# Down projection in seven block products instead of eight, for three of four output pairs of its two groups of eight tiles

## The reference

```python
def swiglu(h, w_gate, w_up, w_down):
    return (jax.nn.silu(h @ w_gate) * (h @ w_up)) @ w_down
...
        x = x + swiglu(rmsnorm(x, norm3_g[l]), w_gate[l], w_up[l], w_down[l])
    return rmsnorm(x, norm_f_g)
```

## Time and profile before

| | us |
|---|---|
| median of 3 runs | 3106.22 |
| lowest, highest | 3101.51, 3106.39 |
| the profiled execution | 3112.17 |
| its span, first to last instruction | 3110.4 |
| PE busy | 2979.9 (96%) |
| DVE, ACT, POOL busy | 1486.7, 945.2, 1407.7 |
| mean granted TensorE clock | 0.977 of 2.4 GHz |
| down projection, first half | 1878.80 to 2124 |
| down projection, second half | 2844.85 to 3084.24 |

### The profile page before, as it was taken

The page is one execution under the profiler, slowest core; times in us unless marked ns, Lnnn a source line. Parts: engine busy times, 40 slices in busy tenths (PEclk is TensorE's granted clock), DMA queues, the critical chain, the costliest instruction groups (busy, mean ns, idle before and its releaser), DMA issues.

```text
span 3110.4 us, 62240 instructions
## 1 busy us (share of the span) xinstructions
PE 2979.9 (96%) x26914; PEld 2543.5 (82%) x26914; DVE 1486.7 (48%) x1859; ACT 945.2 (30%) x1615; POOL 1407.7 (45%) x979
## 2 busy tenths in 40 slices
PE   8999999899888899999999999999999899999997
PEld 7888888788778788987788888887898788888885
DVE  6332633366666642235766661125232866664113
ACT  4123212244444342334333331121232433332111
POOL 4555443335344326236545542246526554543225
PEclk9999999999999979999999999999999999999998
DMA  4433454311212212110322227324111122225512
GB/s 164 163 115 102 161 161 156 114 51 46 59 49 61 63 47 98 35 48 34 120 111 109 108 109 291 129 108 162 41 41 49 73 109 109 114 117 215 222 55 77
DMA packets 168066, 326.14 MB, mean 105 GB/s; under 512 B 46464, under 2 KB 103808, under 8 KB 162176
## 3 DMA queue, kind: packets, MB, share of 16 engines
q1 hardware_dynamic: 167808, 322.38, 29.7%
HBM read 232.15 MB, written 90.18 MB: 104 GB/s over the span
## 4 chain that ended last, share of the span: by engine, by line
PE 72%; DVE 6%; issue 2%; POOL 2%; ACT 1%; SPq 0%; DVEq 0%; DMA 0%; ACTq 0%; POOLq 0%
PE ps L1428 26%; PE ps L1979 25%; PE ps L1931 6%; PE ps L1534 2%; PE ps L1698 2%; PE ps L1700 2%; PE ps L1682 2%; PE ps L1652 1%; DVE tu L2182 1%; PE ps L1779 1%; DVE normed L2699 1%; PE ps L1583 1%; PE ps L1606 1%; PE ps L1638 1%; PE ps L1616 1%
## 5 line engine op out<-in xcount | busy, mean ns | idle before, releaser
L690 POOL TENSOR_TENSOR w_lo<-w_raw,w_hi 128x512 fp32r<-128x512 f32 x296 | 427.9, 1469 | 681.0 <-ACT w_hi L962 679.5
L1428 PE MATMUL ps<-a_hi,w_hi 128*128 128x512 f32 x1152 | 451.3, 392 | 16.3 <-DVE a_lo L2082 9.5
L962 ACT ACTIVATE w_hi<-w_raw 128x512 fp32r<-128x512 f32 x296 | 170.3, 623 | 966.7 <-PE ps L1428 864.4
L1428 PE MATMUL ps<-a_lo,w_hi 128*128 128x512 f32 x1152 | 449.2, 390 | 0.0
L2437 DVE TENSOR_TENSOR x<-ps,x 128x1024 f32<-128x1024 f32 (+1 forms) x80 | 97.9, 1224 | 563.5 <-PE ps L1428 554.0
L1428 PE MATMUL ps<-a_hi,w_lo 128*128 128x512 f32 x1152 | 355.2, 390 | 0.0
L1428 PE MATMUL ps<-b_hi,w_hi 128*128 128x512 f32 x768 | 301.0, 392 | 1.9 <-DVE x L2437 1.9
L1428 PE MATMUL ps<-b_lo,w_hi 128*128 128x512 f32 x768 | 299.8, 390 | 0.0
L1979 PE MATMUL ps<-a_hi,w_hi 128*128 128x512 f32 x672 | 266.6, 397 | 16.3 <-DVE a_lo L2509 8.6
L1428 PEld LDWEIGHTS ps<-a_hi,w_hi 128*128 128x128 f32 x1152 | 216.9, 188 | 63.4 <-DVE a_lo L2082 9.5
L1979 PE MATMUL ps<-a_lo,w_hi 128*128 128x512 f32 x672 | 265.6, 395 | 0.0
(11 more groups left out here) (328 smaller groups left out, 6424.7 us busy)
## 6 DMA issues: line engine op xcount, KB each, us to landing
w_raw<-in_weights SPq DMA_DIRECT2D x228, 512.0 KB, 3.9
hidden<-hid SPq DMA_DIRECT2D x44, 1024.0 KB, 3.9
zT<-z_out SPq DMA_DIRECT2D x44, 512.0 KB, 4.1
w_raw<-kvw SPq DMA_DIRECT2D x32, 512.0 KB, 3.3
a_hi<-hidden SPq DMA_DIRECT2D x28, 512.0 KB, 10.2
a_lo<-hidden SPq DMA_DIRECT2D x28, 512.0 KB, 11.3
suv<-zT SPq DMA_DIRECT2D x16, 512.0 KB, 4.8
x<-in_xT SPq DMA_DIRECT2D x16, 512.0 KB, 5.7
```

Source lines behind the costliest of these rows:

```text
L690: pool.tensor_tensor(low_t[:, u, part, :], w_raw[:, u, part, :], high[:, u, part, :].bitcast(F32), ALU.subtract).then_inc(S["w_lo_done"], 1)
L962: act.activation(split_into(pair)[0][:, u, part, :], w_raw[:, u, part, :], ACT.Copy).then_inc(S["w_hi_done"], 1)
L1428: mm = pe.matmul(to[:, nb, 0:w], wt[:, u, k, :], r[:, k, nb * w:(nb + 1) * w], start=(k == 0 and r is hi_in and wt is w_hi), stop=(k == kn ...
```

## The change

The three seven-product pairs per group come into the down projection, in groups 1 and 2 (g = 0, 1, DOWN = 2). Of the four pairs of a group the first is made as before, plainly, with both tiles side by side (`eights`); the other three by seven products (`sevens`), with bank and operand rules shared with the feed-forward stage (p runs on from 22 to 27). All three groups' tiles are now loaded into `a_hi`/`a_lo`, since the b buffers hold t2, t3, t4; the loads of the next group wait for the second and fourth product of the last pair of the group before.

The blocks are made of raw hidden tiles. For this the first 16 raw tiles are stored from `gate_t` to a new tensor `hidden_raw`, and a pair of raw tiles (j and j + 4 of the group) is loaded into one of two scratch buffers `scr`; `scr0` lies over `hid` and `up_t`, `scr1` over `gate_t`, `u_t` and `p5_t`. `blocks_of(j)` makes four blocks of it on DVE, and the load of j = 2 and 3 waits until the blocks of j - 2 are made. `into_x` adds the seven products up, right into x: nine DVE operations of 512 columns for a pair, in place of two of 1024. The text calls `blocks_of(j)` a unit.

```diff
+        scr = [place(f"scr{i}", [P, 2, TB], F32, OS + (4 + 8 * i) * KB) for i in range(2)]
...
+                if p < sum(FF_GROUPS[:DOWN]):
+                    sp.wait_ge(S["prod"], hf * FF_TILES + p + 1)
+                    sp.dma_start(hidden_raw[p], gate_t[:]).then_inc(S["raw_st"], 16)
...
+                    if j >= 2:
+                        sp.wait_ge(S["t_raw"], since("t_raw", T_RAW * hf + 12 + 16 * g + 4 * (j - 1)))
+                    elif j:
+                        sp.wait_ge(S["st_ev"], ev_all(hf, down_first(g) - 1))
+                    else:
+                        sp.wait_ge(S["hid_st"], since("hid_st", 16 * FF_TILES * (hf + 1)))
+                        if g:
+                            sp.wait_ge(S["t_raw"], since("t_raw", T_RAW * hf + 12 + 16 * g))
+                    f = sum(FF_GROUPS[:g]) + j
+                    for e in range(2):
+                        sp.dma_start(scr[j % 2][:, e, :], hidden_raw[f + e * KT // 2]).then_inc(S[f"scr_in{j % 2}"], 16)
...
+                for g in range(DOWN):
+                    p, d = down_first(g), PAIRS_OUT * g
+                    for j in range(0 if g == 0 else 1, KT // 2):
+                        load_scratch(g, j)
+                    for i in range(2, PAIRS_OUT + 1):
+                        used_up(p + i - 2)
+                        load_down(d + i)
+                    if g + 1 < DOWN:
+                        load_scratch(g + 1, 0)
+                    for k in range(FF_GROUPS[g + 1]):
+                        if k in (0, KT // 2):
+                            sp.wait_ge(S["st_done"], since("st_done", 7 * st(hf, p + DS - 1) + (4 if k else 2)))
+                        load_hidden(hf, g + 1, k)
+                    if g + 1 < DOWN:
+                        load_down(d + PAIRS_OUT + 1)
...
+                    dif_hi(0)
+                    dif_hi(1)
+                    high(p, 1, 5)
+                    dif_hi(2)
+                    dif_hi(3)
+                    act.activation(t2_hi[:], t2_raw[:], ACT.Copy).then_inc(S["t_hi"], 1)
+                    high(p, 2)
+                    copy_1(p)
+                    high(p, 3)
+                    copy_5(p)
+                    high(p, 4)
...
+                    for i in range(DS):
+                        if i:
+                            copy_1(p + i)
+                        if i + 1 < DS:
+                            high(p + i + 1, 0, 6)
+                        if i:
+                            copy_5(p + i)
...
                     product(p, 0, 0)
+                    if first_t is not None:
+                        pe.wait_ge(S["t_lo"], since("t_lo", T_LO * hf + first_t[0]))
                     product(p, 1, 1)
...
+                for g in range(DOWN):
+                    d, p = q_d + PAIRS_OUT * g, down_first(g)
+                    eights(d, g, range(KT), p - 2)
+                    t0 = 7 + 7 * g
+                    sevens(p, (S["st_ev"], ev_all(hf, p - 1)), (t0 + 4, t0 + 5, t0 + 6, t0 + 7))
+                    sevens(p + 1, (S["job_out"], 2 * (d + 1)), None)
+                    sevens(p + 2, (S["st_ev"], ev_all(hf, p)), None)
...
+                            dve.wait_ge(S["raw_st"], since("raw_st", 16 * (hf * 16 + min(p, 16))))
                             op = dve.tensor_tensor(gate_t[:, N1], bank(0), rstd[:, N1], ALU.mult)
...
+                        dve.tensor_tensor(t3_raw[:, j, :], b2[:, N2], b1[:, N2], ALU.subtract).then_inc(S["t_raw"], 1)
+                        if j == 0:
+                            dve.wait_ge(S["values_half"], half_open(hf, p))
+                        dve.tensor_tensor(x_dif[:, j, N2], b1[:, N2], b1[:, N1], ALU.subtract).then_inc(S["t_raw"], 1)
+                        dve.wait_ge(S["t_raw"], since("t_raw", raw0 + 4 * j + 1))
+                        dve.tensor_tensor(t2_raw[:, j, :], t3_raw[:, j, :], b1[:, N1], ALU.add).then_inc(S["t_raw"], 1)
+                        dve.wait_ge(S["t_raw"], since("t_raw", raw0 + 4 * j + 3))
+                        dve.tensor_tensor(t4_raw[:, j, :], b2[:, N1], t2_raw[:, j, :], ALU.subtract).then_inc(S["t_raw"], 1)
...
+                    dve.wait_ge(S["st_done"], since("st_done", 7 * st(hf, p - 1) + 7))
+                    blocks_of(0)
+                    blocks_of(1)
+                    weight_sum_3(p)
+                    weight_sum_1(p)
+                    blocks_of(2)
+                    dif_low(0)
+                    dif_low(1)
+                    blocks_of(3)
+                    dif_low(2)
+                    dif_low(3)
+                    dve.wait_ge(S["t_raw"], since("t_raw", raw0 + 16))
+                    low_block(t2_hi, t2_lo, t2_raw, 11 + 7 * g + 5)
+                    for u in range(2):
+                        add_x(d, u, u, False)
+                    weight_sum_4(p)
+                    weight_sum_2(p)
...
+                    low_block(t3_hi, t3_lo, t3_raw, 11 + 7 * g + 6)
+                    low_block(t4_hi, t4_lo, t4_raw, 11 + 7 * g + 7)
```

More of the change, by code:

```diff
@@ L2060, in _ @@
                     for u in range(2):
[L2061 to L2064 removed]
+                        job(q_e + i, u, *two, n)
             stats_last(4 * HALVES - 1)
@@ L2691, in _ @@
+                q_e = q_d + DOWN * PAIRS_OUT
+                for k in range(KT):
+                    add_x(q_e + k // 2, k % 2, k, True, 2 if k // 2 == 1 else 0)
+                    if hf == 0 and 2 <= k <= KT // 2 + 1:
+                        y_lo(1, range(2 * k - 4, 2 * k - 2))
                 squares_before = (HALVES + 3 * hf + 2) * KT
```

313 lines of the change are left out of this document (214 added, 99 removed).

## The result

| | before | after |
|---|---|---|
| median of the runs, us | 3106.3 (3101.5 to 3117.0, 4 runs) | 3157.4 (3152.9 to 3165.1, 4 runs) |
| ratio, 95% interval | | 1.0162 [1.0128, 1.0196] |
| span of the profiled execution, us | 3110.4 | 3153.3 |
| mean granted clock of TensorE | 0.977 | 0.969 |

The change makes the kernel 1.6% slower, 51 us by the medians and 43 by the profiled executions. Forecast were 3143, so +37, in a range of 3112 to 3172.

The account below looks back on a forecast made before the run. The prediction took TensorE (PE) to bound the down projection, at 0.2267 us a matmul. Gain 32.6 us against opening costs 2 x (22.5 + 12.2) = 69.4 gave +36.8 on 3106.2: 3143 us, range 3112 to 3172.

Parts of the forecast that it names:

- Gain: Down projection, groups 1 and 2: 144 matmuls fewer at 0.2267 us each, 32.6 us gained.
- Feed-forward stores at nothing: Feed-forward stage: storing 16 of 22 raw tiles per half is covered by existing waits and costs 0.
- Transitions and tail at nothing: Passing from sevens to the next group's eights costs 0 (bound 0 to 3 us each); first half's tail unchanged, plus or minus 3.
- Opening of group 1: Scratch loads wait for the last hidden tile's store; product 2 14.4 us late, product 4 18.3 late, before contention.
- contention: In each opening, DVE operations lengthened by POOL's low parts: 2.0 us, bounds 0 and 4.
- openings hidden: Rival: first pair covers most block work if the store lands by about 10 us and loads come early; 3092 us, chance 0.10.
- Opening of group 2: No store in the way; product 2 4.1 us late, product 4 8.0 late, before contention.
- The half clock behind the long wait, hidden: Group 1's opening: products 2 and 3 at half clock end at 46.9 us, before s_4 is ready at 48.2; no added cost.
- the second seven-product pair: Behind each opening, product 4 of that pair waits about 2.2 us for p_t; bounds 0 and 5.
- The sum: Whole kernel: cost 69.4 us less gain 32.6, so +36.8 us.
- The rule weighed: Openings: if DVE and GpSimd exclude each other for whole instructions, contention is 5.2 instead of 2.0, about 13 us more; not adopted.
- the third meeting: In an opening, a POOL operation falling on DVE's low part of t2, counted within the 2.0 us of contention.

Follow-up runs that it names:

- copies_first: Changed kernel with ACT taking copies u_t and p_t ahead of roundings in the second and third seven-product pair; 3152.3 us, ratio 1.0126.
- stores_only: Kernel before the change plus only the stores of 16 of 22 raw hidden tiles in each half; 3117.0 us, ratio 1.0015.
- early_loads: Changed kernel with group 1's scratch loads 0 and 1 in earlier-free buffers, ahead of the last hidden tile's store; 3155.6 us, ratio 1.0132.
- no_loads: Changed kernel without scratch loads, blocks made from tiles already in SBUF (products not the real ones); 3129.4 us, ratio 1.0067.
- copies_sums: copies_first, with DVE also making weight sums s_4 and s_2 ahead of the first pair's additions into x; 3149.5 us, ratio 1.0111.
- two_plain: Changed kernel with two plain pairs per group, a separate tile for x differences, and reordered copies and VectorE work; 3094.1 us, ratio 0.9945.

## Why the prediction was right, and where its terms were off

The time fell in the range, and PE's waits in the openings came where they were foretold, ended by what was foretold. The longest was 17.3 us, the 14.4 and 2.0 of the forecast and a little more; group 2's first was 6.5, above the 4 to 6 named as its sign. One term of the sum was half of what it should have been.

**Gain.** 144 matmuls at 0.2267: right. Without a stall, 216 matmuls took 49.05 us (copies_first), the pitch of the earlier trace rows.

**Feed-forward stores at nothing.** Right: the stretch takes 407.0 us in stores_only and 406.6 in the changed kernel, against 407.0.

**Transitions and tail at nothing.** Right: PE's timeline shows no wait at the start of groups 2 and 3, and group 3 with its tail takes what it took.

**Opening of group 1.** Forecast (from the chain's start): unit 0 at 24.1, product 2 at 38.9 and 2.0 for contention, product 4 at 50.2. Measured 24.2, 41.7 and 50.9. The landing came out to 0.1 us, and two block operations took 1.75 in place of 0.68, 2.1 us together. The remaining 0.7 is there when unit 2 starts, at 31.8 in place of 31.1: load 1, which the forecast had ready in time, was waited for by 0.81 us, and load 2 came later with it. The reading behind it was half right. The last tile's store was in the way, as said; but early_loads shows that the load would have been late without it, by the tile loads that the earlier trace rows shows, and I had not said so. The rival "openings hidden" asked for a store landing at 10 us and for loads ahead of need; the traces let the price be split. Of the 17.3 us by which product 2 of group 1 is late, the place behind the store is 4.7 (early_loads), the rest of the loads 6.4 (to no_loads), and what no_loads keeps is 6.1.

**Opening of group 2.** Forecast product 2 6.1 and product 4 10.0 us late (4.1 and 8.0, and 2.0 for contention), measured 6.4 and 10.2. The way there is as told too: unit 0 ends at 12.9 (forecast 13.0), load 1 is there at 16.7 (17.1), and two block operations take 1.78 and 1.65 us.

**The half clock behind the long wait, hidden.** Right: behind the long wait the clock is at half for most of products 2 and 3 (first window below), and product 4 comes 9.16 us behind product 2 against 9.3, of which PE waited 1.31. In copies_sums, where s_4 is ready earlier, that wait is gone and product 4 comes 7.86 us behind product 2.

**The term that was off: the second seven-product pair.** Forecast 2.2 us, for a wait for p_t alone; measured 4.2 to 4.3 in each of four groups. ACT's order put u_t behind high parts too, which gave a wait of 1.78 us that I hadn't seen. Four times 2.1 is 8.4 of the 10.1 us by which the four groups exceed the forecast (46.9 against 36.8). copies_first, which takes just these two waits away, shortens the groups by 16.1. The bounds of the term were 0 and 5, and 4.3 is inside them.

**The sum.** Groups +46.9, the rest -4, against +36.8 forecast. The other 8 us up to the median's +51 lie between profiled executions and medians of four runs, and nothing here explains them. By the medians the forecast was 14 us short of 51.

**The rule weighed.** In no_loads VectorE and GpSimd worked beside each other for a longer piece: operations that take 0.68 and 1.30 us alone took 1.77 and 1.74 there, one of each per 1.7 us. The Trainium skill, SBUF — State Buffer, "Who interferes with whom", has a VectorE instruction with two SBUF inputs contend with a GpSimd one that reads SBUF; the trace agrees. It calls the sharing an exclusive lock, but "for the whole instruction", which the prediction takes from it, is said there of two-port modes. A meeting costs VectorE about 1.07 us (0.96 to 1.10), as the longest L2548 of the earlier trace rows had it, and not the 1.3 of a whole GpSimd operation. What kept the term small in the change is that two operations of an opening met one; in no_loads it was four, and by the 6.9 us of its low parts four in group 1 of two_plain too. The sum was right to stay at 2 us, by the count, which the forecast had taken from the order of work (GpSimd's low parts of operands 1 and 5 fall on unit 2); its price of 0.9 was a little low, and the third meeting that it named, with the low part of t2, cost VectorE nothing (2.29 us, as alone).

## What to carry to other kernels

A form that needs fewer matmuls pays for its operands' making at every place where it starts anew. Walk the chain from the load to the first product that needs it, and compare it with the work that can stand in front; here 42 us of chain stood against 24 of cover, and of the kernels run only the one with a second plain pair turned the loss of 1.6% into a gain of 0.55%. Before moving a load forward in a queue, look at the DMA share of the stretch: at 1.0 what is in front has to go through first, and most of the wait that the load loses turns up as time under way (here it gained 4.8 us). And in an engine that works in order, list every copy that PE's next products wait for ahead of roundings that have slack: 4 us a group hung on it.

## What the runs showed of the hardware

**DMA.** In early_loads the queue moved 414 GB/s for 19.5 us, for the most part loads from HBM, with one core running. The Trainium skill, DMA: Bandwidth & Descriptors, "Where 436 GB/s comes from", says that for transfers between HBM and SBUF the HBM side, some 358 GB/s, binds; it gets that figure by dividing a stack's rate by two cores, and sets beside it a load measured at 425. With one core running the trace goes past the first and is near the second.

**TensorE's clock.** Waits of about 1.8 us, twice within 5 us, left the clock at 2.4 GHz in group 2 (granted 1.00 behind either); in group 1 it fell to 1.2 GHz behind a single wait of 1.78 us, some 28 us after the long one. Windows of the changed kernel: behind the wait of 17.26 us, behind that of 1.78 in group 1, and at the same place of group 2.

```profile
1916.40:1922.40 6.00, 5.91 (x17) 4.68 (x18) 4.82 (x5) 2.11 (x3) 2.94 (x1) 0.62 0.00 0
...
1944.00:1948.80 4.80, 4.61 (x12) 3.25 (x12) 1.43 (x3) 1.66 (x4) 3.13 (x3) 0.64 0.50 202
...
2037.50:2042.30 4.80, 3.06 (x12) 2.17 (x12) 1.63 (x3) 1.64 (x4) 3.15 (x3) 1.00 0.51 199
```

In group 1 the slower products used up the wait that group 2 had next (0.21 in place of 1.75 us), so both ended 4.3 us late. In early_loads the two groups of the first half lost 4.2 and 4.3 us in this pair (53.12 and 53.24 us from product 4 of the pair before to the group's end), and the two of the second half, where the clock fell behind the second wait (0.61 and 0.68 in some 4.5 us after it), 5.9 (54.86 and 54.88). Of the eight such pairs of waits in these two kernels the clock fell behind the first in three, behind the second in two, and behind neither in three. Which it is differs from group to group, and no run here explains it.
